# Squares of the input on ScalarE, one attention step a block, and a mixer schedule of three tiles a visit

## What is computed

```python
# first block
h = rms_norm(x, norm_gain); proj = h @ w_in          # q,k,v,gates of the attentions A, B, C and the gates gm
ya = diff_attention(qa, ka, va)                      # A: two softmaxes a head, a difference
yb = sliding_window_attention(qb, kb, vb, sinks)     # B
yc = forgetting_attention(qc, kc, vc, logf)          # C: decay from a running sum of log forget gates
x = x + (sum of gate_i * (y_i * silu(g_i)) @ w_up_i) @ w_o
# second block
h = rmsnorm(rms_norm(x)); z = h @ w_in_2             # a_u, a_gate, b_q, b_f, b_v, b_g, c_b, c_c, c_v
y_a = rglru: conv, gates r and i, a = exp(log_a), linear scan, times gelu(a_gate), norm by head
y_b = hgrn2: f = sigmoid(b_f), k = 1 - f, q = silu(b_q); decayed causal attention; norm by head; times silu(b_g)
y_c = c_b * conv(c_c * c_v), norm by head
x = x + [y_a, y_b, y_c] @ w_out; x = x + conv_ffn(rmsnorm(x)); x = x + sigmoid(x @ w_gate) * (p @ w_proj)
out = rmsnorm(x)
```

## Time and profile before

| what | value |
|---|---|
| time, median of 3 runs | 1281.94 us (1281.29 to 1286.49) |
| profiled execution: its own time | 1284.15 us |
| profiled execution: span from first to last instruction | 1282.3 us |
| mean granted TensorE clock | 0.987 |
| busy: TensorE, DVE, ScalarE, GpSimd | 97%, 51%, 43%, 51% |

### The profile page before, as it was taken

How to read it: one execution, slowest core, us unless ns; L and a number is a source line. 1 busy time by engine, 2 the same in 40 slices (tenths; PEclk the granted TensorE clock), 3 DMA queues, 4 the chain that set the end, 5 groups by cost and what they waited for, 6 DMA issues and landing times.

```text
span 1282.3 us, 17066 instructions
## 1 busy us (share of the span) xinstructions
PE 1244.9 (97%) x6230; PEld 984.4 (77%) x6230; DVE 650.4 (51%) x1217; ACT 553.6 (43%) x1066; POOL 659.3 (51%) x501
## 2 busy tenths in 40 slices
PE   7998989999999999999989999999999999999996
PEld 5886767777778888888776776878888888788885
DVE  6436844665542412125267546459999999200024
ACT  4444535677544332335552647542322333322344
POOL 4772223244336544446455464646767776655542
PEclk9999999999999999999998999999999999999998
DMA  5333212113223333353222121423333333433321
GB/s 198 106 115 100 73 50 74 50 50 83 59 67 90 107 91 99 89 158 109 74 82 62 42 71 47 122 76 89 99 99 99 88 94 86 125 98 92 101 74 66
DMA packets 63939, 113.94 MB, mean 89 GB/s; under 512 B 7016, under 2 KB 12776, under 8 KB 63856
## 3 DMA queue, kind: packets, MB, share of 16 engines
q1 hardware_dynamic: 63712, 112.84, 30.7%
q10 hardware_dynamic: 144, 0.00, 0.0%
HBM read 110.71 MB, written 2.11 MB: 88 GB/s over the span
## 4 chain that ended last, share of the span: by engine, by line
PE 85%; DVE 7%; ACT 4%; issue 2%; POOL 2%; DMA 1%; DVEq 0%; SPq 0%; ACTq 0%; POOLq 0%
PE pb L906 25%; PE pb L907 24%; PE pb L909 24%; PE pb L1060 2%; PE pb L1036 1%; PE pb L1011 1%; POOL HL L2186 1%; PE pb L1025 1%; PE pb L974 1%; POOL wlo L2186 1%; DVE U L1639 1%; PE pb L976 1%; PE pb L975 1%; DVE sq L1627 1%; ACT L1231 1%
## 5 line engine op out<-in xcount | busy, mean ns | idle before, releaser
L2186 POOL TENSOR_TENSOR wlo<-raw,whi 128x512 fp32r<-128x512 f32 (+3 forms) x398 | 539.8, 1370 | 443.0 <-ACT whi L1242 442.6
L906 PE MATMUL pb<-HH,whi 128*128 128x512 f32 x968 | 393.9, 407 | 0.0
L907 PE MATMUL pb<-HL,whi 128*128 128x512 f32 x968 | 383.3, 396 | 0.0
L909 PE MATMUL pb<-HH,wlo 128*128 128x512 f32 x968 | 382.2, 395 | 0.0
L1242 ACT ACTIVATE whi<-raw 128x512 fp32r<-128x512 f32 (+3 forms) x398 | 235.1, 611 | 180.5 <-PE pb L909 152.6
L906 PEld LDWEIGHTS pb<-HH,whi 128*128 128x128 f32 x968 | 182.9, 189 | 51.8 <-issue 9.8
L909 PEld LDWEIGHTS pb<-HH,wlo 128*128 128x128 f32 x968 | 182.4, 188 | 42.5
L907 PEld LDWEIGHTS pb<-HL,whi 128*128 128x128 f32 x968 | 182.7, 189 | 41.1 <-issue 2.4
L1639 DVE SCALAR_TENSOR_TENSOR cv<-zf,vecs,cv 128x512 f32<-128x512 f32 x88 | 124.8, 1419 | 3.1
L1630 DVE TENSOR_TENSOR X<-pb,X 128x512 f32<-128x512 f32 x24 | 16.6, 691 | 137.7 <-PE pb L909 137.3
L1769 DVE CUSTOM_DVE_ANT_0 P<-pb,B 128x256 f32<-128x256 f32 (+3 forms) x96 | 43.6, 454 | 68.1 <-PE pb L1011 39.2
(11 more groups left out here) (386 smaller groups left out, 1924.4 us busy)
## 6 DMA issues: line engine op xcount, KB each, us to landing
raw<-in_wall SPq DMA_DIRECT2D x362, 256.0 KB, 2.7
raw<-in_wall SPq DMA_DIRECT2D x16, 192.0 KB, 2.4
raw<-in_wall SPq DMA_DIRECT2D x8, 260.0 KB, 3.0
X<-in_xT SPq DMA_DIRECT2D x8, 256.0 KB, 5.5
N<-c_sums SPq DMA_DIRECT2D x8, 256.0 KB, 3.9
X<-in_xT SPq DMA_DIRECT2D x2, 1024.0 KB, 7.6
outT<-PP SPq DMA_DIRECT2D x8, 256.0 KB, 2.2
raw<-in_wall SPq DMA_DIRECT2D x12, 128.0 KB, 2.1
```

Of the source, the lines that this page charges most:

```text
L906: pe.do.matmul(b, hi, xh[k], start=start, stop=False)
L907: pe.do.matmul(b, hi, xl[k], start=False, stop=False)
L909: m = pe.do.matmul(b, lo, xh[k], start=False, stop=stop)
L2186: g.do.tensor_tensor(lo, x, hi.bitcast(F32), ALU.subtract).then_inc(*up(name, point))
```

## The change

It has five parts. (1) The squares of the input in `first(k)` go from DVE to ScalarE, which squares `xk[k]` right behind the high half; the step `lambda` moves from before the kC tiles to behind `columns1`. (2) The loop over A's values makes one attention step after each block instead of one and two in turn. (3) In the mixer a visit of `hgrn_steps` does a level for all three tiles; visits come at fixed blocks (k = 2, 5, 7 of the bv tiles, then i = 3 and 7 of a tile), gates at i = 1 and 5; hgrn's head norms come at once behind its last values, among the cv tiles. (4) `base` is split: the `Ln` (`logs`) and the copy `base_far` stand ahead of the bq tiles, the log sums and the exponentials (`inverse`) between them, `queries` becomes `query(t)` for each tile, and `base_near` follows the first level; `base_k` lies in `G3`. (5) From the mixer on, banks are taken by `take_any`, the bank least recently given or released, with `keep` and `release`.

```diff
+    def take_any(self, tile, keep=False):
+        bank = min((b for b in range(8) if b not in self.kept), key=lambda b: self.held.get(b, -1))
+        self.hold(bank, tile)
+        if keep:
+            self.kept[bank] = tile
...
-    def tick(self, i=1):
-        if i % 2:
-            self.ticks += 1
-            if self.ticks % 2:
-                self.advance(self.gates)
+    def tick(self, i=None):
+        if i in (1, 5, None):
+            self.advance(self.gates)
+        if i in (3, 7, None):
             self.advance(self.heads)
...
-        add("lambda")
         for m in range(4):
             take("main", ("kC", m))
...
         add("columns1")
+        add("lambda")
         add("out", "qC", 0)
...
             add("vA", k)
-            for _ in range(1 + k % 2):
-                self.step()
+            self.step()
...
         for t in range(3):
             add("forget", t)
+        add("decays")
+        add("logs")
+        add("base_far")
         for t in range(3):
-            self.tile("x5", ("bq", t), "win2")
+            tile("bq", t)
             if t == 0:
-                take("x5", ("columns2",))
+                take(("columns2",))
                 add("columns2")
+                add("log_sums")
             add("bq_out", t)
-
-        def gates_steps():
-            add("decays")
-            add("queries")
-            yield
-            add("base")
-            yield
+            release(("bq", t))
+            if t == 1:
+                add("inverse")
+            add("query", t)
+            add("level", 4, t)
...
             add("bv", k)
-            if k in (0, 1, 3):
+            if k in (2, 5, 7):
                 self.advance(self.heads)
...
-        while self.gates:
+        while self.gates or self.heads:
             tick()
         for t in range(3):
-            self.tile("m3", ("bg", t), "win2", tick)
-            add("bg_out", t)
+            tile_out("bg", t, tick)
+            if t:
+                add("head_out", 2 + t)
             residual()
...
     def hgrn_steps(self):
-        for p in range(3):
-            add("level", 4, p)
-        yield
         for h in (8, 16, 32, 64):
             for p in range(3):
...
                 add("hg_scores", h, p)
                 add("level", h, p)
-                yield
+            if h == 8:
+                add("base_near")
+            yield
...
         add("far_values", 256, 2)
         yield
+        add("squares_b")
+        yield
+        yield from self.head_norms([[3, 4], [5]])
...
             def first(k):   # ScalarE
                 a.do.activation(mh[k], xk[k], ACT.Copy, scale=vecs("norm_gain", k)).then_inc(*up("xhi", ("m_hi", k)))
+                if k > 2:
+                    a.wait_ge(*at("sq_step", k - 2))
+                a.do.activation(sqs[(k - 1) % 2] if k else acc, xk[k], ACT.Square).then_inc(*up("a_norm", ("sq", k)))
...
-            def base():     # ScalarE
+            def logs_of():
                 tables(LNEXP)
                 a.wait_ge(*at("f", 2))
                 a.do.activation(logs[:, :], F3[:, :], ACT.Ln).then_inc(*up("a_hg", ("logf",)))
-                a.wait_ge(*at("qd", 4))
...
+                tables(EXPTANH)
+
+            def inverse():
                 a.wait_ge(*at("log_sums"))
...
+            def query(t):
+                a.wait_ge(*at("qd", 4, t))
+                a.do.activation(blocks(third(base_q, t), 4)[:, :, 1, :], blocks(third(qd3, t), 4)[:, :, 1, :], ACT.Copy,
+                                scale=2.0 ** BALANCE).then_inc(*up("a_hg", ("base_q_far", t)))
...
             def level(h, p): # DVE
                 if h == 4:
-                    v.wait_ge(*at("base_q_far"))
+                    v.wait_ge(*at("base_q_far", p))
```

More of the change, by code:

```diff
@@ L168, in take, with release @@
         self.hold(banks[n % len(banks)], tile)
+    def take_any(self, tile, keep=False):
[3 more added lines that the diff above has]
+            self.kept[bank] = tile
+    def release(self, tile):
+        del self.kept[self.bank[tile]]
+        self.clock += 1
+        self.held[self.bank[tile]] = self.clock
     def hold(self, bank, tile):
@@ L172, in hold @@
         self.before[tile] = self.holder.get(bank)
-        self.held[bank] = len(self.bank)
+        self.clock += 1
+        self.held[bank] = self.clock
         self.holder[bank] = tile
@@ L462, in second @@
             add("ag_out", t)
[L463 to L474, removed]
-                yield
+            release(("ag", t))
+        self.mixed = {3, 4, 5}
         def norm_steps():
-            add("squares_b")
-            yield
             add("squares_a")
@@ L513, in second @@
             for half in range(2):
-                take("all", ("ffn", half, j))
+                take(("ffn", half, j))
                 self.proj(("ffn", half, j), "ffn_up", 2816 * half + P * j)
                 if j == 0 and half == 0:
-                    take("all", ("norm3",))
+                    take(("norm3",))
                     add("norm3")
@@ L522, in second @@
         for d in range(8):
-            take("all", ("down", d))
+            take(("down", d))
             self.proj(("down", d), "ffn_dn", P * d, range(NPAIR))
@@ L526, in second @@
         for d in range(8):
-            take("all", ("pp", d))
+            take(("pp", d))
             self.proj(("pp", d), "ple_p", P * d, range(2))
@@ L530, in second @@
         for d in range(6):
-            take("all", ("pg", d, 0))
+            take(("pg", d, 0))
             self.proj(("pg", d, 0), "ple_g", P * d)
@@ L538, in half_tile @@
         def half_tile(half, d):
-            take("all", ("pg", d, half))
+            take(("pg", d, half))
             add("half_tile", half, d)
@@ L545, in second @@
         half_tile(1, 6)
-        take("all", ("norm4", 0))
+        take(("norm4", 0))
         add("half_out", 0)
@@ L564, in hgrn_steps @@
                     for s in range(2):
-                        take("x5", ("hg", h, s, p))
+                        take(("hg", h, s, p), keep=True)
                 add("hg_scores", h, p)
                 add("level", h, p)
[L568 to L572, removed]
+                if p == 2 or h == 64 and p == 1:
+                    for s in range(2):
+                        release(("hg", h, s, p if h == 64 and p == 2 else 0))
+            if h == 8:
+                add("base_near")
+            yield
+        for ps in ((0,), (1, 2)):
+            for p in ps:
+                for s in range(2):
+                    take(("base", p, s))
+                add("base_scores", p)
             yield
@@ L1486, in rg_decay @@
                 a.wait_ge(*at("rg_slope"))
+                a.wait_ge(*at("full", ("base", 2, 1)))
                 a.wait_ge(*last("a_gate"))
```

158 lines of the change are left out of this document (91 added, 67 removed).

## The result

The changed kernel takes 1285.52 us (median of 20 runs, 1283.14 to 1287.11) against 1282.86 for the kernel before in the same comparison (20 runs, 1278.2 to 1286.49). The ratio is 1.0019, 95% interval 1.0011 to 1.0027: by the ratio 2.4 us slower, within the 0.5% that I called no change. The prediction was 1265.6, 20 us lower.

What follows compares the result with a forecast made beforehand. TensorE, busy 97% of the span, bounds the kernel, so only its waits and the half clock behind them can be won. Opening 5.5, A's values 4.3 and mixer 6.5 make 16.3 us off 1281.94: 1265.6 us, range 1257 to 1275.

Steps and rivals of the forecast that it cites:

- The opening: Start of the kernel, kC tiles: TensorE's wait for weight splits and the lost clock go, 5.5 us won (bounds 4.0 and 6.2).
- A's values: Loop over A's values: the transposes' 2.84 us wait for DVE and the low clock behind go, 4.3 us won.
- The mixer: Mixer: 12.3 us of old waits and clock won, less 1.8, 2.0 and 2.0, net 6.5 (bounds -1 and 12.5).
- The 12.3 us of old waits: Mixer: bv's 4.6 us wait, the 64-span scores' 2.6 and 5.05 of clock behind them, all to go.
- The span-8 wait: First level's scores in the bv tiles: a new TensorE wait for DVE's `qd`, 1.3 us, taken as 1.8.
- The late chain at the ag tiles: Bg and ag tiles: TensorE waits for a late weight split, 2.0 us lost, and 2.0 for clock behind either new wait.
- The head norms: Mixer: hgrn's early head norms cost nothing, squares, sums and scalings being hidden by 5.5 us of matmuls a tile.
- The clock: Whole kernel: each TensorE wait of 2.5 us and more is followed by a stretch at 1.2 GHz.
- The sum: Whole kernel: 5.5 + 4.3 + 6.5 = 16.3 us less, from 1281.94 to 1265.6 us.
- Rival 2: Bg and ag tiles: ScalarE becomes the late engine through table loads; 5 us more give 1271 to 1272; chance 0.19.
- The condition I wrote for being wrong: Changed trace: a new wait reaches 5 us, a wait shows in cc or cv, or C's start (3.2 us) grows.

Runs made afterwards that it cites:

- experiment 8: On experiment 4's kernel, the `lambda` step moved behind the eviction of C's values: 1270.33 us, ratio 0.9892 to the kernel before.
- experiment 1: Kernel before with the opening's edits alone (input squares on ScalarE, `lambda` behind `columns1`): 1281.78 us, ratio 0.9977.
- experiment 3: Changed kernel with the opening and A's values put back as before, so the mixer's edits alone: 1292.64 us, ratio 1.0072 to the kernel before.
- experiment 4: Changed kernel with the table set `LNEXP` named ahead of head norms k = 0, 3 and 5: 1273.2 us, ratio 0.992 to the kernel before.
- experiment 5: Changed kernel with `LNEXP` named only ahead of the first late head norm (k = 0): 1277.85 us, ratio 0.9952 to the kernel before.
- experiment 10: Kernel before with the call naming `LNEXP` in `squares_b` taken away: 1298.38 us, ratio 1.0121.
- experiment 9: On experiment 8's kernel, hgrn's three early head norms moved behind the square root, set named once ahead and once behind: 1265.72 us, ratio 0.9868 to the kernel before.
- experiment 2: Kernel before with one attention step a block of A's values and nothing else: 1277.98 us, ratio 0.9958.

## Why the prediction was wrong, by its own steps

- **The opening, 5.5.** kC's sums came at 30.6, as said, 5.7 earlier, with a clock of 1 and no wait near 20, and the first matmul came 0.5 later (I had 0.65). The step that failed is the sentence that `lambda` costs "under 1 us ... hidden by the matmuls of the second qC tile". It took 3.2 us on DVE (38.6 to 41.8), beside GpSimd's splits, and what stood behind it was the chain that evicts the queries and scales the input, block by block, with GpSimd. That chain has no slack up to C's values: with `lambda` behind them the wait there is 0.3 and not 2.4 (experiment 8). Worth 3.0 by time (experiment 1), not 5.5.
- **A's values, 4.3.** Right: 4.4 in the trace, 5.4 (3.7 to 7.1) by time.
- **The mixer, net 6.5.** It lost 9.2 (experiment 3). The 12.3 us of old waits were right: both waits went, as said. What failed is what I put against them, 5.8 us, in the next three terms.
- **The span-8 wait, 1.8 (bounds 0 and 4).** 3.7, with a granted clock of 0.91 over the window. Mechanism right, size off: between two `query` steps the hand-over took 5.2 us and not 4 (`qd` of the thirds ends at 634.3, 639.4 and 644.6 in experiment 4).
- **The late chain at the ag tiles, 2.0, and 2.0 for the clock.** Mis-sized by the count of loads: I counted seven from the cc to the bg tiles, and the trace has ten from 716 to 739. I had taken one load for a norm's two functions. Waits of 1.8, 0.6 and 3.9 came of it (0.6 and 3.9 are the 4.6 of the table), already at the bg tiles.
- **The head norms, "at nothing".** This is the step that decided. I followed the three early norms and did not ask what naming the set at the old place had done for the five norms that stayed. They got ten loads (12.8 us) where one had stood, the wait of 8.5, and a clock of 0.81: 8.6 us of the stretch (experiment 5). Naming the set at all three places gives 13.2 us back of the 15.7 between forecast and result, and taking the one call out of the kernel before costs 15.5 (experiment 10).
- **The clock.** I wrote that each wait of 2.5 us and more is followed by a stretch at 1.2 GHz. The waits of 3.0 and 3.1 at one place in experiments 5 and 4, with a clock of 0.71 and 0.60 behind the first and 1.00 behind the second, show that a wait's length alone does not settle it. The clock terms were guesses of that kind.
- **The sum.** 1265.6 is also what experiment 9 takes (1265.7). That is luck, and no credit to the sum: that kernel names the set, holds `lambda` elsewhere and has the three early norms in another place. With only the tables named the kernel stands at 1273.2, at the upper end of the range.
- **The rivals.** Rival 2 was the right mechanism, ScalarE late by table loads, at 5 us more; the loads took 13.2 (789.1 to 775.9 in the stretch), since I looked only at the bg and ag tiles. The condition I wrote for being wrong, a new wait of 5 us or more, was met by one I had not placed anywhere.

What stays open: the 3.4 us of late head sums that are still in experiment 9 (1.7 and 1.7), and whether the chain between the level visits can be shortened. Neither moving the visits nor moving the low parts did it. Open too is how much of experiment 9 is loads and how much is order.

## What to carry to other kernels

A call that sets a state of an engine (here the activation set) serves everything behind it in that engine's list. When a step is moved, ask what its side effects did for the steps that stay, and count the state changes over the whole list, before and after, from the trace or from the list. In this kernel an `Ln` and an `Exp` in turns cost two loads a pair (2.6 us) unless the set with both is named ahead of them, and one edit that looks free can then be worth more than all the waits it was meant to remove.

## What the hardware showed that I had not expected

The same DVE dot product over 128x64 elements took 0.22 us with GpSimd idle and 1.35 us with GpSimd splitting weights beside it, six times as long; before's row, to be read beside those of after at 38.61 and 39.90:

```profile
26.32 0.22 DVE L1664 CUSTOM_DVE_ANT_0 th<-vecs 128x64 f32<-128x64 f32 x1
```

The rows suggest that it ends when GpSimd's instruction does: the two subtractions from 38.57 take 1.3 each, and the dot products end at 39.96 and 41.23; in experiment 8 they took 0.37 and 1.32, and end at 67.06 and 68.31, 0.1 behind two GpSimd instructions (66.98 and 68.24). No run tried this by itself. In these rows a short DVE step moved to where GpSimd works is not short any more. And two executions of the same code differ by 1.3 us at the same point, before any edit acts: the first matmul behind C's values starts at 73.01 in the kernel before and at 71.66 in experiment 2, with a granted clock from 30 to 40 of 0.82 and 0.96. Offsets below 2 us between two traces say nothing by themselves.
